# One encoder block on one core: token blocks of 512 with plain products, or chunks of 1024 with Strassen products and mixers that read their inputs back from memory

## What is computed

```python
h = rmsnorm(x, g_pre)
proj = h @ w_in                      # 1024 x 7440 columns, split into:
# q_a, k_a (512 each), v_a (1024), lr_a (16), z_a (1024), q_b (1024), k_b, v_b (128 each), z_b, m_a, m_b (1024 each)
log_a = log_sigmoid(lr_a @ w_decay_up + b_decay_up) / 16
# branch A, 4 heads of 128 x 256, per chunk of 64 tokens:
#   S = S * exp(b_last) + (k * exp(b_last - b))^T v;  o = q S        (b: running sum of log_a)
y_a = (rmsnorm(o_a, g_gla) * silu(z_a)) @ w_branch_gla
# branch B, 16 heads of 64, 2 key heads, rotary, window of 2 chunks, a sink per head:
#   o = softmax([q k^T / 8, sink])[:-1] v
y_b = (o_b * silu(z_b)) @ w_branch_swa
y = sigmoid(m_a + b_a) * y_a + sigmoid(m_b + b_b) * y_b
out = x + rmsnorm(y @ w_out, g_post)
```

## Time and profile before

| | |
|---|---|
| median of 3 runs | 2180.45 us (2180.06 to 2182.92) |
| profiled execution | span 2179.4 us from the first to the last instruction; its own time lies within the runs above, about 1 us over its span |
| PE busy | 2114.9 us, 97% |
| PEld, DVE, ACT, POOL busy | 1813.8, 956.7, 749.2, 1008.3 us |
| DMA | 208.85 MB, 96 GB/s on average |

### The profile page before, as it was taken

One profiled execution on the slowest core, in us unless ns is written; L12 is line 12 of the kernel. 1 busy time (PEld: TensorE's weight loads), 2 busy tenths in 40 slices (PEclk: granted clock), 3 DMA queues, 4 the chain that ended last, 5 costly groups with the idle time before them and its releaser, 6 DMA issues.

```text
span 2179.4 us, 35654 instructions
## 1 busy us (share of the span) xinstructions
PE 2114.9 (97%) x13536; PEld 1813.8 (83%) x13536; DVE 956.7 (44%) x1837; ACT 749.2 (34%) x1055; POOL 1008.3 (46%) x567
## 2 busy tenths in 40 slices
PE   6999999999999999999999999999999999999995
PEld 5888878889888988788988798878898879887885
DVE  5245544442534454534253446452444445535334
ACT  6422233333532233333352222333335222333332
POOL 2445533654334653365343464346534346444553
PEclk9999999999999999999999999999999999999998
DMA  4222222333322222233332222223333222222332
GB/s 141 78 78 78 78 87 79 118 105 126 118 88 69 87 89 78 69 136 98 125 118 78 78 85 77 81 78 135 124 111 107 78 76 81 81 84 78 135 129 94
DMA packets 57359, 208.85 MB, mean 96 GB/s; under 512 B 6672, under 2 KB 6816, under 8 KB 57184
## 3 DMA queue, kind: packets, MB, share of 16 engines
q1 hardware_dynamic: 54640, 197.40, 27.5%
q0 software_dynamic: 2544, 9.05, 1.1%
HBM read 197.97 MB, written 8.39 MB: 95 GB/s over the span
## 4 chain that ended last, share of the span: by engine, by line
issue 54%; POOL 39%; DVE 2%; PE 2%; DMA 1%; POOLq 1%; ACT 0%; SPq 0%; ACTq 0%; DVEq 0%
POOL w_lo L1249 30%; POOL g_lo L1285 4%; PE pu L484 2%; POOL y_lo L1289 2%; POOL q_rope L1313 1%; DMA w_raw<-in_w 1%; DVE rows L935 1%; POOL k_rope L1325 1%; POOL kd_lo L1300 1%; DVE rows L1225 0%; POOLq L1242 0%; DVE out_stat L1216 0%; ACT w_hi L715 0%; PE pm L448 0%; POOL w_hi L1246 0%
## 5 line engine op out<-in xcount | busy, mean ns | idle before, releaser
L1249 POOL TENSOR_TENSOR w_lo<-w_raw,w_hi 128x1024 fp32r<-128x1024 f32 x313 | 759.3, 2429 | 841.8 <-ACT w_hi L715 840.7
L497 PE MATMUL pu<-h_hi,w_hi 128*128 128x512 f32 x1152 | 456.7, 396 | 0.2 <-DVE w_lo L893 0.2
L497 PE MATMUL pu<-h_hi,w_lo 128*128 128x512 f32 x1152 | 449.1, 390 | 0.0
L497 PE MATMUL pu<-h_lo,w_hi 128*128 128x512 f32 x1152 | 448.8, 390 | 0.0
L715 ACT ACTIVATE w_hi<-w_raw 128x1024 fp32r<-128x1024 f32 x340 | 357.4, 1053 | 254.7 <-PE pu L484 98.9
L484 PE MATMUL pu<-w_hi,h_hi 128*128 128x256 f32 x1408 | 403.3, 286 | 0.0
L484 PE MATMUL pu<-w_lo,h_hi 128*128 128x256 f32 x1408 | 398.2, 283 | 0.0
L484 PE MATMUL pu<-w_hi,h_lo 128*128 128x256 f32 x1408 | 398.0, 283 | 0.0
L484 PEld LDWEIGHTS pu<-w_hi,h_hi 128*128 128x128 f32 x1408 | 269.6, 191 | 13.6 <-issue 9.9
L484 PEld LDWEIGHTS pu<-w_lo,h_hi 128*128 128x128 f32 x1408 | 269.7, 192 | 0.5
L484 PEld LDWEIGHTS pu<-w_hi,h_lo 128*128 128x128 f32 x1408 | 269.8, 192 | 0.0
(11 more groups left out here) (180 smaller groups left out, 2864.7 us busy)
## 6 DMA issues: line engine op xcount, KB each, us to landing
w_raw<-in_w SPq DMA_DIRECT2D x340, 512.0 KB, 3.7
x_in<-in_x SPq DMA_DIRECT2D x20, 512.0 KB, 6.7
x_res<-in_x SPq DMA_DIRECT2D x16, 512.0 KB, 5.1
out_y<-rows POOLq DMA_DIRECT2D x16, 512.0 KB, 3.8
gpost_sb<-in_gpost POOLq DMA_DIRECT2D x2, 256.0 KB, 6.5
totals<-sums SPq DMA_DIRECT2D x16, 4.0 KB
const_sb<-in_consts SPq DMA_DIRECT2D x1, 146.0 KB, 2.2
wdecay_sb<-in_w_decay POOLq DMA_DIRECT2D x1, 128.0 KB, 2.8
```

The costliest lines, as they stand in the source:

```text
L497: last = mm(bank[:, :], b[:, k, j * P:(j + 1) * P], a[:, k, :], start=(k == 0 and n == 0), stop=(k == KD - 1 and n == 2))
L1249: TT(w_lo[c % 2][:, ks, :], w_raw[half][:, :, :], as_f32(w_hi[c % 2][:, ks, :]), ALU.subtract).then_inc(w_lo_ok.sem, 1)
```

## The change

The kernel is written anew around the same arithmetic.

- **Chunks.** Two passes of 1024 tokens (`SB`) instead of four of 512, unrolled, without hardware loops. All products are column-major: 128 weight columns by 512 tokens.
- **Slots and groups.** A slot is one product of a 512 x 128 piece of weights with a 512 x 512 piece of tokens: 4 x 3 = 12 matmuls. A group is 256 columns by 1024 tokens over the full depth of 1024. In a plain group that takes 8 slots. In a fast group (`fast`, the 29 groups of h in a pass, less the very first) Strassen's scheme (the Winograd form) makes it of 7 slots. That is 57 fast and 25 plain groups, 599 slots.
- **What the scheme adds.** Sums of weight quarters on DVE (`col_sums`: T3, T1, T2, T4, four 128x512 operations for each fast group), sums of token quarters once in a pass (`head_sum`, `HPREP`), and sums of partial results: `u2` (a copy on ScalarE, then an addition on DVE) and the four result tiles `ct0` to `ct3`, which DVE adds up from `u2` and the banks. Product 3 of a group uses bank 1 again, and so waits for `u2_ok`; product 5 adds onto bank 1 and waits for `c_ok3`.
- **Results go to memory.** Every result tile `ct` is stored to DRAM, 256 KB each. The rotation is done in SBUF on `ct` and two tables, three 128x512 operations on DVE and three on POOL for each half of a `kvB` or `qB` group (before, DVE read the bank and POOL had one sum to form). The mixers load q, k, v, the decays and z back in jobs of 128 tokens (`SWA`, `GLA`, 16 of each in a pass, one each 5 and 4 slots), and store their outputs, which come back as split token operands (`fill`).
- **Mixers.** q and k of branch B need no transposes now; k and v of branch A do (`key_transposes`, 192 transposes in all). The state update is done in float32 instead of three float32r passes.
- **Start and end.** The sums of squares of x are made on TensorE, by matmuls with a column of ones, and both halves are done before the first product. The result is written transposed, 16 tiles of 128x512 at the very end, each with a sum on POOL.

The core of the diff (of 3,060 lines):

```diff
-TB = 512
-NB = SEQ // TB
+SB = 1024
+NSB = SEQ // SB
+HT = SB // 2
...
+FAST_ORDER = ("B11", "T2", "T1", "T3", "B21", "T4", "B22")
+FAST_TOKENS = ("A11", "S2", "S1", "S3", "A12", "A22", "S4")
+PLAIN_ORDER = ("B11", "B21", "B12", "B22")
...
+NWB = 7
+HI_AHEAD, LO_AHEAD = 5, 4
...
+DECAY = {12 + 3 * t: t for t in range(NT)}
+SWA = {47 + 5 * n: n for n in range(16)}
+GLA = {130 + 4 * n: n for n in range(16)}
...
+            def product(s):
...
+                bank_wait(g, i)
+                n = OPERAND_NO[g.n, col] % NWB
+                bank = pu[bank_of(g, i)]
+                for j in range(KH):
...
+                    for k, (wgt, tok) in enumerate(((w_hi, a_hi), (w_hi, a_lo), (w_lo, a_hi))):
+                        ins = mm(bank[:, :], wgt[n][:, j, :], tok[place][:, j, :],
...
+                    if i == 1:
+                        dve.wait_ge(prod_ok, s + 1)
+                        dve.wait_ge(p1_ok, n + 1)
+                        TT(u2[:, :], u2[:, :], pu[1][:, :], ALU.add).then_inc(u2_ok, 1)
+                    elif i == 2:
...
+                        TT(ct[3][:, :], u2[:, :], pu[2][:, :], ALU.add).then_inc(u4_ok, 1)
+                    elif i == 3:
...
+                        TT(ct[3][:, :], ct[3][:, :], pu[1][:, :], ALU.add).then_inc(c_ok[3], 1)
+                    elif i == 5:
...
+                        TT(ct[2][:, :], u2[:, :], pu[1][:, :], ALU.add).then_inc(c_ok[2], 1)
+                        if g.kind in ROPED:
+                            rope(g, 1)
+                    elif i == 6:
...
+                        TT(ct[1][:, :], u2[:, :], pu[2][:, :], ALU.add).then_inc(c_ok[1], 1)
+                        if g.kind in ROPED:
+                            rope(g, 0)
...
+                TT(tmp[0][rows, :], x2[rows, :], sin, ALU.mult).then_inc(rope_d_ok, 1)
+                dve.wait_ge(rope_p_ok, number + 1)
+                link(TT(x1[rows, :], x1[rows, :], cos, ALU.mult))
+                TT(x1[rows, :], x1[rows, :], tmp[0][rows, :], ALU.subtract).then_inc(f_ok[2 * half], 1)
...
+                TT(tmp[1][rows, :], x1[rows, :], sin, ALU.mult).then_inc(rope_p_ok, 1)
+                pool.wait_ge(rope_d_ok, number + 1)
+                TT(x2[rows, :], x2[rows, :], cos, ALU.mult).then_inc(pool_seq, 1)
+                pool.wait_ge(pool_seq, number + 1)
+                TT(x2[rows, :], x2[rows, :], tmp[1][rows, :], ALU.add).then_inc(f_ok[2 * half + 1], 1)
```

More of the change, by code:

```diff
@@ L45 @@
[L45 to L52, removed]
@@ new lines @@
+NGS = len(ORDER)
+NH = 29
+Group = namedtuple("Group", "n sb kind idx fast at size")
+GROUPS = []
+for _sb in range(NSB):
+    for _n, (_kind, _idx) in enumerate(ORDER):
+        _fast = _n < NH and not (_sb == 0 and _n == 0)
+        _at = GROUPS[-1].at + GROUPS[-1].size if GROUPS else 0
+        GROUPS.append(Group(len(GROUPS), _sb, _kind, _idx, _fast, _at, 7 if _fast else 8))
+NG = len(GROUPS)
+NS = GROUPS[-1].at + GROUPS[-1].size
+SLOT = [(g, i) for g in GROUPS for i in range(g.size)]
+BASE = [GROUPS[sb * NGS].at for sb in range(NSB)]
@@ new lines, with at, step @@
+YBASE = [GROUPS[sb * NGS + NH].at for sb in range(NSB)]
+def at(s):
+    return SLOT[s] if 0 <= s < NS else (None, -1)
+def step(s, r):
+    g, i = at(s - r) if s >= r else (None, -1)
+    return g if i == 0 else None
+FAST = [g.n for g in GROUPS if g.fast]
+ROPED = ("kvB", "qB")
+STORED = [g.n for g in GROUPS if g.kind not in ("yB",) and not (g.kind == "out" and g.sb == NSB - 1)]
+FINISHED = [g.n for g in GROUPS if g.fast and g.kind not in ("qk", "v")]
+ROPES = [g.n for g in GROUPS if g.kind in ROPED]
@@ new lines @@
+FILL_NO = {(f.sb, f.what, f.name): f.n for f in FILLS}
+NHEAD = 8
+SPLIT_AT = {f.split: f for f in FILLS if f.split >= 0}
+TABLES = 9
+BLOB = 6
+LR = (10, 11)
+DECAY = {12 + 3 * t: t for t in range(NT)}
+VT_AT = GROUPS[1].at
+SWA = {47 + 5 * n: n for n in range(16)}
+GLA = {130 + 4 * n: n for n in range(16)}
+SUMS = 2
+SQUARES = {61 + 2 * t: t for t in range(NT)}
+RSTD = 79
+RB = {83: 0, 88: 1}
+HPREP = {92 + 24 * j: j for j in range(KH)}
+NORM = {92 + 6 * x: x for x in range(16)}
+GATE_BUFS = 2
@@ new lines, with __init__, take, tile @@
+NCOLS = sum(COLS.values())
+LRW0 = 512
+LATER0 = LRW0 + 12 * 6 * RANK
+NBLOB = LATER0 + P
+NBLOB_OUT = 9
+class Block:
+    def __init__(self, nc, start):
+        self.nc, self.top = nc, start
+    def take(self, nbytes):
+        start = self.top
+        self.top = start + (nbytes + 31) // 32 * 32
+        return start
+    def tile(self, name, shape, dt, start=None):
+        nbytes = 4 * int(np.prod(shape[1:]))
+        return self.nc.alloc_sbuf_tensor_at(name, list(shape), dt,
+                                            offset=self.take(nbytes) if start is None else start)
```

2525 lines of the change are left out of this document (1428 added, 1097 removed).

## The result

The changed kernel takes 2263.58 us (median of 4 runs, 2262.18 to 2264.24) against 2180.49 of the kernel before: 1.0379 times as long, 95% interval 1.0364 to 1.0393. It is slower by 3.8%; the forecast was 2110. The profiled execution spans 2262.4 us.

What follows compares the result with a forecast made beforehand. TensorE, busy 97% of the span, was taken as the bound: 45 start + 1632 products + 281 rest + 18 lag + 60 rotations + 15 clock + 30 chains + 28 end = 2109 span, so 2110 us; range 2015 to 2195.

Steps and rivals of the forecast that it cites:

- start: Before the first product: loads of x, squares, sums, scalings and copies take 45 us, bounds 36 and 55.
- products: On TensorE, 7188 matmuls of 512 columns at 0.227 us each: 1632 us, 192 less than before.
- rest of TensorE: TensorE's mixers, transposes and low-rank product, with the pauses at block turns gone: 281 us.
- first group's lag: Behind the start, the first fast group waits for sums of h, splits and angle work: 18 us (0 to 30).
- rotations, at `u2`: In ten rotated groups TensorE stands still 6 us each, product 3 waiting for the late `u2` addition: 60 us.
- clock: After each of ten pauses the lowered TensorE clock loses 1.5 us: 15 us.
- short chains: Mixer pieces keep their distances in shorter slots; 32 + 32 + 16 jobs at 0.4 us: 30 us (0 to 103).
- end: Last tile's copies and sums, POOL adding 16 tiles, and the final store: 28 us.
- DVE and POOL: Two-input SBUF operations on DVE queue with POOL's, one at a time; hidden in usual groups, 6 us late in rotated ones.
- the rival with 6.8 us at 1.2 GHz per pause: Every TensorE pause costs 6.8 us at the lower clock: 2110 + 19 = 2129 us; chance 0.12.
- memory at nothing: Spilling and reading back, about 316 MB instead of 209, costs nothing, hidden by 3 or 4 slots from load to use.
- Rival 2: Hand-over late in every fast group, products 3 and 5 waiting for drains; 47 more groups lose 2.6 us: 2232; chance 0.14.

Runs made afterwards that it cites:

- run 3: Changed kernel with the second mixer's probability transposes, value products and gating one slot later on all engines: 2191.33 us, 1.0047 of the kernel before.
- run 13: Changed kernel with VectorE's division of the probabilities moved ahead of the drain, TensorE's order untouched: 2201.90 us, 1.0098 of the kernel before.
- run 5: Changed kernel with each decay's sums on TensorE, and the exponentials behind them, one slot later: 2245.56 us, 1.0299 of the kernel before.
- run 8: Changed kernel with decay sums and second mixer one slot later, squares ahead of copies, and decays four slots apart instead of three: 2138.53 us.
- run 12: Changed kernel with each decay's logarithm replaced by a second exponential, sparing ScalarE's table changes (decay values wrong): 2246.96 us, 1.0299 of the kernel before.
- run 7: Changed kernel with only GpSimd's three operations of each half rotation cut to 32 of 512 columns: 2210.07 us, 1.0128 of the kernel before.
- run 9: Changed kernel with all six operations of each half rotation on VectorE, none on GpSimd: 2235.96 us, 1.0251 of the kernel before.
- run 10: Changed kernel with second mixer and decay sums a slot later, decays every four slots, squares ahead of copies, rotations on VectorE alone: 2126.05 us.
- run 11: Changed kernel with useless matmuls ahead of TensorE's waits, 12 per `la_lo` and 8 per `prob`: 2396.70 us, 1.099 of the kernel before.

## Why the prediction was wrong

The sum, term by term (forecast, then the changed kernel):

| term | forecast | measured |
|---|---|---|
| start | 45 | 55 |
| products | 1632 | 7188 x 0.227 = 1632 |
| rest of TensorE | 281 | 292, what is left of the span |
| first group's lag | 18 | 13 (wait for `ct`, L1212) |
| rotations, at `u2` | 60 | 0 |
| clock | 15 | 66 |
| short chains | 30 | 148 (`la_lo` 70.3, `prob` 69.4, `kd` 8.4) |
| other waits | 0 | 27 (`issue` 10.5, `u` 7.2, `ct` L1560 5.8, and 3.5) |
| end | 28 | 29 |

The clock's 66 is an estimate: 240 us at 0.50, less 25 of them behind the last product and 72 in waits ahead of it, leave 143, at 0.46 each. The low level of the first 59 us isn't in it; it is in the start.

**The step that failed** is in "DVE and POOL" and "Shorter chains": "Product 3 of the next group waits for it and is due 4 slots after the start", taken as the first thing to be late behind a rotation, with the decays' and scores' work put beside it as mere extra load, and the chain of the scores priced by its three slots, "about 9.3 us". That the piece in the queue behind a rotation is the next mixer's, due sooner than `u2`, was not looked up in VectorE's order. Nor was the second, wider error: of three slots only the last is open to a piece that stands behind a drain, and its own work there (3.4 us in the job shown: 1.2 + 0.2 + 2.0), with the drain and a sum of weight quarters ahead of it, is more than one slot. In place of 60 us of waits at `u2` the runs showed none there, and 140 us at `la_lo` and `prob`. Runs 3 and 13 show the cause for `prob` from two sides: a slot more (72 us) or another place in the queue at the same distance (62 us); in both the division also meets GpSimd less often, and no run parts the two effects. For the decays run 5 with 8 shows it less cleanly, for 34 us of waits stay, 24 of them in three places; that their late start too is a matter of the queue is read from the timeline and from run 12, and no run moved their place alone.

**The rotations** were priced nearly right and put at the wrong place. 10 x 6 us at `u2` and 15 for the clock were forecast; cutting them short brings 78 us, clock included. That the two agree is luck: the waits that went were other ones. A half rotation takes 5.3 us, not 6.0. The alternation, one engine at a time, is seen in `ct` at 1.76 us beside GpSimd in place of 0.69, and runs 7 and 9 bear it out. The Trainium skill, page "SBUF — State Buffer", section "SBUF: two separate sides", says of an operation of VectorE with two inputs in SBUF and one of GpSimd that reads SBUF that whichever starts first holds their shared ports for its whole instruction; the trace agrees here.

**The clock** was put more than four times too low. Its mechanism was named, and the rival with 6.8 us at 1.2 GHz per pause was right in kind; but ten pauses were counted where there were 16 + 27. The Trainium skill's page "TensorE: Matmul & The Clock Gate", section "HAM oscillation", counts half of the time at the low level as lost. By it the clock cost 108 us of the 215 ahead of the last product, an estimate; the trace gives less, since 72 of the 215 lie in waits.

**Right** were the step of the products and with it the gain of the scheme (a fast group without waits takes seven slots), the end, the first group's lag, and memory at nothing: 330 MB moved, and TensorE waited 0.3 us for a load in all. The start was 10 us too short. Each half has 32 float32 matmuls for its sums of squares, shown as 64 records of 0.22 us, the price that the forecast gave them at half clock; but they follow one another without a gap for 13.8 us, and ScalarE's squares wait for them. The forecast counted only the 8 behind the last squares, 4 us. **Rival 2**, the only one above 2200, came nearest to the time (2232, 32 too low), by luck, for its mechanism isn't there: no wait spreads over all fast groups.

So the scheme is not what makes the changed kernel slow. With the distances set for its shorter slots, the rotations on VectorE and the squares ahead of the copies (run 10) it is 2.5% faster than before.

## What to carry to other kernels

When a schedule counts in slots and a slot gets shorter, check each piece on each engine for the slots that are open to it: from the end of the last wait that stands ahead of it in its queue to the moment it is due, with its own work at the length that it has beside the engine it contends with. Price many short waits of TensorE with the clock behind them: here 188 us of waits between the first product and the last, 140 of them the two named, brought some 66 more, an estimate from the steps. And a slot gained at the consumer may be lost again where a buffer is handed back, as at `log_a`.

## What the runs showed that was not expected

- A rotation is faster on VectorE alone (six operations) than shared with GpSimd (three each): 4.75 us for a half against 5.33, and 28 us for the kernel with its ten rotated groups, run 9.
- A float32 matmul of 512 columns took 0.88 us, the float32r one 0.227 (run 11); 64 records of two-column float32 sums took 13.8 us at the start. The granted clock reads 1.00 there, but the lengths are those of the low level.
- Useless matmuls ahead of TensorE's waits raised its mean granted clock from 0.947 to 0.969 and took 92 us off the time at 1.2 GHz, 33 of them in waits (run 11). They are no remedy by themselves: they cost more than that here.
- Of the 240 us at the low level in the changed kernel 81 lie in waits of TensorE. A mean granted clock prices only the rest.
